# Embedding LayerNorm of a two-layer block: statistics of a token tile in one VectorE pass, tile 0 scaled on ScalarE, one low part on GpSimd

## The reference, cut

```python
def layernorm(x, g, b):
    mu = jnp.mean(xf, axis=-1, keepdims=True)
    var = jnp.mean(jnp.square(xf - mu), axis=-1, keepdims=True)
    y = (xf - mu) * lax.rsqrt(var + LN_EPS) * g + b
...
def hybrid_layer(x, ...):
    proj = x @ w_in
    ...
    return layernorm(DEEPNORM_ALPHA * x + out, ln_g, ln_b)

def first_block(x, ...):
    h = layernorm(x, emb_ln_g, emb_ln_b)
    for l in range(DEPTH):
        h = hybrid_layer(h, ...)
    return h
...
```

## Time and profile before

| | |
|---|---|
| time, median of 3 runs | 2583.37 us (2583.27 to 2583.72) |
| the profiled execution | 2582.42 us |
| its span, first to last instruction | 2580.6 us |
| TensorE busy | 2559.9 us (99%) |
| VectorE busy | 1781.2 us (69%) |
| ScalarE busy | 1360.2 us (53%) |
| GpSimd busy | 16.7 us (1%) |
| DMA queue, share of 16 engines | 52.1% |
| granted TensorE clock, mean | 1.00 |

### The profile page before, as it was taken

The page is one execution under the profiler, slowest core; times in us unless marked ns, Lnnn a source line. Parts: engine busy times, 40 slices in busy tenths (PEclk is TensorE's granted clock), DMA queues, the critical chain, the costliest instruction groups (busy, mean ns, idle before and its releaser), DMA issues.

```text
span 2580.6 us, 39874 instructions
## 1 busy us (share of the span) xinstructions
PE 2559.9 (99%) x14224; PEld 2213.4 (86%) x14224; DVE 1781.2 (69%) x2712; ACT 1360.2 (53%) x2112; POOL 16.7 (1%) x20
## 2 busy tenths in 40 slices
PE   7999999999999999999999999999999999999999
PEld 6888888888888888888888887888888888888888
DVE  8787658777658766556666765678767665666655
ACT  5665565565566444444444554775544444444444
POOL 2000000000000000000000000000000000000000
PEclk9999999999999999999999999999999999999999
DMA  7554455454554555555554564444555545555454
GB/s 296 185 190 177 181 211 228 153 189 177 183 208 163 195 195 178 181 201 191 193 191 164 183 212 163 147 148 170 185 192 186 195 168 189 211 183 193 174 183 164
DMA packets 75435, 482.41 MB, mean 187 GB/s; under 512 B 8384, under 2 KB 10816, under 8 KB 30784
## 3 DMA queue, kind: packets, MB, share of 16 engines
q1 hardware_dynamic: 75328, 481.00, 52.1%
HBM read 477.82 MB, written 2.10 MB: 186 GB/s over the span
## 4 chain that ended last, share of the span: by engine, by line
PE 83%; DVE 1%; ACT 1%; issue 0%; ACTq 0%; DVEq 0%
PE acc L808 45%; PE acc L809 23%; PE acc L814 3%; PE acc L816 3%; PE acc L815 3%; PE score L808 1%; PE score L1080 1%; PE score L809 1%; PE head_ps L1103 0%; DVE low L1527 0%; PE turn_ps L1089 0%; PE head_ps L1104 0%; PE sums L1023 0%; ACT high L1159 0%; ACT L1438 0%
## 5 line engine op out<-in xcount | busy, mean ns | idle before, releaser
L808 PE MATMUL acc<-xs,high 128*128 128x512 f32 x4000 | 1400.6, 396 | 2.5 <-DVE xs L2011 2.3
L1527 DVE TENSOR_TENSOR low<-raw,high 128x1024 fp32r<-128x1024 f32 (+2 forms) x976 | 1079.8, 1124 | 453.4 <-ACT high L1159 429.7
L1159 ACT ACTIVATE high<-raw 128x1024 fp32r<-128x1024 f32 (+2 forms) x976 | 945.2, 976 | 506.3 <-PE acc L809 375.7
L809 PE MATMUL acc<-xs,low 128*128 128x256 f32 x4000 | 1111.2, 278 | 0.0
L808 PEld LDWEIGHTS acc<-xs,high 128*128 128x128 f32 x4000 | 750.3, 188 | 178.2 <-DVE xs L2011 3.2
L809 PEld LDWEIGHTS acc<-xs,low 128*128 128x128 f32 x4000 | 751.7, 188 | 0.6
L808 PE MATMUL acc<-hidden,high 128*128 128x512 f32 x1408 | 490.8, 395 | 0.1
L1198 ACT ACTIVATE lowsum<-acc 128x256 f32<-128x256 f32 x348 | 133.5, 384 | 520.7 <-PE acc L809 520.0
L809 PE MATMUL acc<-hidden,low 128*128 128x256 f32 x1408 | 391.2, 278 | 0.0
L808 PEld LDWEIGHTS acc<-hidden,high 128*128 128x128 f32 x1408 | 264.1, 188 | 62.7 <-DVE low L1527 0.4
L809 PEld LDWEIGHTS acc<-hidden,low 128*128 128x128 f32 x1408 | 264.6, 188 | 0.0
(11 more groups left out here) (374 smaller groups left out, 2017.9 us busy)
## 6 DMA issues: line engine op xcount, KB each, us to landing
raw<-w_up_dram SPq DMA_DIRECT2D x176, 1024.0 KB, 4.8
raw<-w_down_dram SPq DMA_DIRECT2D x128, 704.0 KB, 4.0
raw<-w_in_dram SPq DMA_DIRECT2D x78, 1024.0 KB, 4.8
raw<-w_out_dram SPq DMA_DIRECT2D x32, 1024.0 KB, 4.8
raw<-w_heads_dram SPq DMA_DIRECT2D x24, 1024.0 KB, 4.8
raw<-w_mixout_dram SPq DMA_DIRECT2D x16, 1024.0 KB, 4.8
raw<-w_mem_dram SPq DMA_DIRECT2D x8, 1024.0 KB, 4.8
raw<-w_nat_dram SPq DMA_DIRECT2D x8, 1024.0 KB, 4.8
```

The costliest lines, as they stand in the source:

```text
L808: eng.matmul(bank_, hi, moving, start=start, stop=False)
L809: return eng.matmul(bank_[:, S:2 * S], lo, moving[:, 0:S], start=False, stop=stop)
L1159: eng.activation(high[:, s % SPLIT, to:to + n * P], raw[:, s % RAW, at_:at_ + n * P], ACT.Copy).then_inc((highs_a, highs_b)[piece], 1)
L1527: eng.tensor_tensor(low[:, s % SPLIT, w], raw[:, s % RAW, at_:at_ + n * P], high[:, s % SPLIT, w].bitcast(F32), ALU.subtract).then_inc((lo ...
```

## The change

**Statistics.** VectorE makes mean and variance of a token tile with four `bn_stats` over 512 features each and one `bn_aggr` (`row_moments`); sums, squares and shift are gone from it and from ScalarE. This is done for tile 0 first, up to reciprocal and bias, then for tile 1.

**Scaling.** All four chunks of tile 0 are scaled on ScalarE (`scaled`) while VectorE works on tile 1. Of tile 1, chunks 0 and 1 (`FIRST_ON_DVE`) are scaled on VectorE, the second of them after the affines of bank 1, and chunks 2 and 3 on ScalarE. TensorE transposes the halves of chunks 0 and 1 that belong to tile 0 as soon as they and `par` are there, and the halves of tile 1 after them (`turn_tile`, `turn_first`).

**One low part on GpSimd.** The first piece of slab 1's low part (`low[:, 1, 0:1024]`) is made by GpSimd as its first work, after both first high pieces. It is counted in a semaphore of its own, `emb_low`, for which TensorE waits ahead of the second product (`b` = 0, slab 1). `lows_a` isn't raised for it: the first low piece of slab 2 waits for `emb_low` and raises `lows_a` by 2.

```diff
-ACC_AT = {"emb": 0, "memory": 4, "ln0": 12, "ln1": 30, "memory_heads": 48}
+ACC_AT = {"memory": 0, "ln0": 8, "ln1": 26, "memory_heads": 44}
+FIRST_ON_DVE = 2
...
@@ -890,8 +894,12 @@
                                 eng.wait_ge((lows_a, lows_b)[b // 8], s + n + 1)
                         elif n == 0:
                             wait_split(eng, split_norm(r.name), b)
-                            if b % 8 == 0:
+                            if b % 8 == 0 and (r.name, b) == ("in_a0", 0):
+                                eng.wait_ge(lows_a, 1)
+                            elif b % 8 == 0:
                                 eng.wait_ge((lows_a, lows_b)[b // 8], s + 2)
+                        elif (r.name, b) == ("in_a0", 0):
+                            eng.wait_ge(emb_low, 1)
                         last = product(banks[n], high[:, (s + n) % SPLIT, at_], low[:, (s + n) % SPLIT, at_],
                                        in_mix(r)[:, b, :], b == 0, b == KT - 1)
                         if n:
@@ -1120,11 +1128,11 @@
             def turn_chunk(name, c):
 
                 n = LAYER_NORMS.index(name)
-                if name == "emb" and c == 0:
-                    eng.wait_ge(par_in, 16)
-                eng.wait_ge(z_done, 5 * n + c + TB)
+                if name == "emb":
+                    return turn_first(c)
+                eng.wait_ge(z_done, FIRST_ON_DVE + 5 * (n - 1) + c + TB)
                 if c:
-                    eng.wait_ge(z_second, 3 * n + c)
+                    eng.wait_ge(z_second, 4 - FIRST_ON_DVE + 3 * (n - 1) + c)
                 for j in (2 * c, 2 * c + 1):
                     if j >= 4:
 
@@ -1136,8 +1144,34 @@
                                                  z[:, b, kt * P:(kt + 1) * P], ident)
                     last.then_inc(turned_x, 1)
...
+            def turn_tile(c, b):
+
+                for j in (2 * c, 2 * c + 1):
+                    for m in range(2):
+                        kt = 2 * j + m
+                        last = eng.transpose(turn_banks[j % 4][:, m * S + b * P:m * S + (b + 1) * P],
+                                             z[:, b, kt * P:(kt + 1) * P], ident)
+                    if b:
+                        last.then_inc(turned_x, 1)
+
+            def turn_first(c):
+
+                if c >= 2:
+                    eng.wait_ge(split_l, split_count("emb", 4 * (c - 2) + 3))
+                    eng.wait_ge(emb_first, c + 1)
+                    turn_tile(c, 0)
+                if c < FIRST_ON_DVE:
+                    eng.wait_ge(z_done, c + 1)
+                else:
+                    eng.wait_ge(z_second, c + 1 - FIRST_ON_DVE)
+                turn_tile(c, 1)
+
             def between(name):
                 if name == "in_a0":
+                    eng.wait_ge(par_in, 16)
+                    for c in range(2):
+                        eng.wait_ge(emb_first, c + 1)
+                        turn_tile(c, 0)
                     turn_chunk("emb", 0)
                     turn_chunk("emb", 1)
@@ -1264,18 +1298,22 @@
                     eng.wait_ge(unit_there, 1)
                 eng.activation(dummy[:, :], unit[:, :], ACT.Sqrt)
                 if name == "emb":
-                    whole_squares()
+                    eng.wait_ge(emb_var, 1)
+                    eng.activation(ln_root[:, 0:1], ln_var[:, 0:1], ACT.Sqrt).then_inc(emb_root, 1)
+                    eng.wait_ge(emb_scaled, 1)
+                    for c in range(4):
+                        scaled(0, name, c).then_inc(emb_first, 1)
+                    eng.wait_ge(variance, N_OF[name] + 1)
+                    eng.activation(ln_root[:, 1:2], ln_var[:, 1:2], ACT.Sqrt).then_inc(root, 1)
+                    split_high(0, r, 0, None)
+                    split_high(0, r, 1, None)
+                    eng.wait_ge(par_in, 16)
...
...
+            def scaled(b, name, c):
+                w = slice(512 * c, 512 * (c + 1))
+                return eng.activation(z[:, b, w], token_major(name)[:, b, w], ACT.Identity, bias=ln_bias[:, b:b + 1],
+                                      scale=ln_inv[:, b:b + 1])
+
             def second_scaled(name, c):
                 eng.wait_ge(ln_scaled, LAYER_NORMS.index(name) + 1)
-                w = slice(512 * c, 512 * (c + 1))
-                eng.activation(z[:, 1, w], token_major(name)[:, 1, w], ACT.Identity, bias=ln_bias[:, 1:2], scale=ln_inv[:, 1:2])\
-                    .then_inc(z_second, 1)
-
-            def whole_squares():
-                for n in range(2 * TB):
-                    b, w = n // 2, slice(n % 2 * D // 2, (n % 2 + 1) * D // 2)
-                    eng.wait_ge(x_in[n], 16)
-                    eng.wait_ge(x_first, b + 1)
-                    eng.activation(z[:, b, w], x_tok[:, b, w], ACT.Square, bias=ln_shift[:, b:b + 1],
-                                   accum_out=ln_sums[:, 8 + n:9 + n]).then_inc(accumulated, 1)
+                scaled(1, name, c).then_inc(z_second, 1)
@@ -1493,6 +1526,9 @@
                 steps_done += 1
                 eng.wait_ge(pool_order, steps_done)
 
+            eng.wait_ge(highs_a, 2)
+            eng.tensor_tensor(low[:, 1, 0:8 * P], raw[:, 1, 0:8 * P], high[:, 1, 0:8 * P].bitcast(F32),
+                              ALU.subtract).then_inc(emb_low, 1)
...
                 eng.wait_ge((highs_a, highs_b)[piece], val(s + 1, 4, i))
+                both = (s, piece) == (2, 0)
+                if both:
+                    eng.wait_ge(emb_low, 1)
                 eng.tensor_tensor(low[:, s % SPLIT, w], raw[:, s % RAW, at_:at_ + n * P], high[:, s % SPLIT, w].bitcast(F32),
-                                  ALU.subtract).then_inc((lows_a, lows_b)[piece], 1)
+                                  ALU.subtract).then_inc((lows_a, lows_b)[piece], 2 if both else 1)
...
                 c = N_OF[name]
                 if name == "emb":
-                    whole_sums()
-                    eng.tensor_reduce(ln_total[:, 0:TB], ln_sums[:, 0:8].rearrange("p (n c) -> p n c", c=4), AX.X,
-                                      ALU.add).then_inc(x_sums, 1)
-                    eng.wait_ge(x_sums, 1)
-                    eng.tensor_scalar(ln_offset, ln_total[:, 0:TB], -1.0 / D, None, ALU.mult)
-                    step_(eng.scalar_tensor_tensor(out=ln_mean, in0=ln_total[:, 0:TB], scalar=1.0 / D, in1=ln_shift,
-                                                   op0=ALU.mult, op1=ALU.add))
-                    step_(eng.tensor_tensor(ln_square, ln_mean, ln_mean, ALU.mult))
-                    eng.wait_ge(accumulated, accumulations(name, 2 * TB))
-                    step_(eng.tensor_reduce(ln_total[:, TB:2 * TB], ln_sums[:, 8:12].rearrange("p (n c) -> p n c", c=2), AX.X,
-                                            ALU.add))
-                    step_(eng.tensor_scalar(ln_var, ln_total[:, TB:2 * TB], 1.0 / D, LN_EPS, ALU.mult, ALU.add))
-                    eng.tensor_tensor(ln_var, ln_var, ln_square, ALU.subtract).then_inc(variance, 1)
-                    eng.wait_ge(root, c + 1)
-                    step_(eng.reciprocal(ln_inv, ln_root))
-                    eng.tensor_tensor(ln_bias, ln_offset, ln_inv, ALU.mult).then_inc(ln_scaled, 1)
+                    for b in range(TB):
+                        row_moments(b)
+                        one = slice(b, b + 1)
+                        eng.tensor_scalar(ln_var[:, one], emb_stat[:, b, 1:2], LN_EPS, None, ALU.add)\
+                            .then_inc((emb_var, variance)[b], 1)
+                        step_(eng.tensor_scalar(ln_offset[:, one], emb_stat[:, b, 0:1], -1.0, None, ALU.mult))
+                        eng.wait_ge((emb_root, root)[b], 1)
+                        step_(eng.reciprocal(ln_inv[:, one], ln_root[:, one]))
+                        eng.tensor_tensor(ln_bias[:, one], ln_offset[:, one], ln_inv[:, one], ALU.mult)\
+                            .then_inc((emb_scaled, ln_scaled)[b], 1)
                     return
@@ -1967,22 +2000,17 @@
             def z_chunk(name, c):
 
                 w = slice(512 * c, 512 * (c + 1))
-                for b in range(1 if c else TB):
+                for b in [1] if name == "emb" else range(1 if c else TB):
                     eng.tensor_scalar(z[:, b, w], token_major(name)[:, b, w], ln_offset[:, b:b + 1], ln_inv[:, b:b + 1],
                                       ALU.add, ALU.mult).then_inc(z_done, 1)
 
-            def whole_sums():
-                for n in range(4 * TB):
-                    b, c = n // 4, n % 4
+            def row_moments(b):
+                for c in range(4):
                     if c % 2 == 0:
-                        eng.wait_ge(x_in[n // 2], 16)
-                    ins = eng.tensor_reduce(ln_sums[:, n:n + 1], x_tok[:, b, 512 * c:512 * (c + 1)], AX.X, ALU.add)
-                    if c == 0:
-                        step_(ins)
-                        eng.tensor_scalar(ln_shift[:, b:b + 1], ln_sums[:, n:n + 1], -1.0 / 512, None, ALU.mult)\
-                            .then_inc(x_first, 1)
```

(11 more changed lines are left out.)

16 lines of the change are left out of this document (7 added, 9 removed).

## The result

The changed kernel takes **2593.46 us** in the median of its runs (2589.99 to 2608.87, and one launch of 13.8 ms, which is an outlier and not counted below), the kernel before 2583.37 beside it. The ratio is 1.0041, 95% interval 1.0027 to 1.0056: slower by 10 us (0.4%), where 2581.9 was forecast and 2580.9 to 2584.0 was the range. The profiled execution of after took 2590.99, its span is 2589.2.

The account below looks back on a forecast made before the run. TensorE was taken as the bound, busy 2559.9 of 2580.6 us, with gains only from its early stops; -1.5 for `b` = 8 and 0 elsewhere took the median from 2583.37 to 2581.9, range 2580.9 to 2584.0.

Parts of the forecast that it names:

- Sum. -1.5 for `b` = 8, 0 for `rows`, 0 for the rest: Whole kernel: the terms added up, taking the profiled execution from 2582.42 to 2580.9 and the median to 2581.9 us.
- `b` = 8: TensorE's product after its last early stop: to start at 26.1 instead of 27.60, 1.5 us earlier.
- `rows`: Load queued behind slab 5: issued at 31.4, landing at 44.5, VectorE waiting 4.1 us, 0.6 slack before TensorE's tile 5.
- the zero for the rest: Everything besides the start and the `rows` load: claimed to change the time by 0.
- My rivals: Four other outcomes: late `rows` 0.16, slow GpSimd part 0.12 or 0.02 with a load, slow first products 0.08, slow BN_STATS 0.03.
- rival 3: TensorE slow at its first products, eight pairs taking twice 2.9 us, 0.9 of it hidden: 2583.9; chance 0.08.
- Statistics: VectorE's embedding norm: each BN_STATS 0.69 us, and the root moving from 12.1 to 11.4.
- ScalarE: Second high part held by its DMA until 13.1, ending at 14.2 as before; affines start at 14.1, not 14.95.
- First product: TensorE's first product at 16.9 instead of 18.09, with 0.2 added for contention with GpSimd.
- GpSimd's part: Low part of slab 1 from 14.3, bounds 2.9 to 5.1 us, taken as 3.3; second product waits 0.3.
- Rival 4: BN_STATS no gain at 1.38 us each, first product near 21.5: 2586.7; chance 0.03.

Follow-up runs that it names:

- experiment 5: Four kernels that shift where tiles lie in memory, compared with the kernel before: ratios 1.0084, 1.0002, 1.0008 and 1.0044.
- tiles_unused: The kernel before with the two small tiles (224 bytes) allocated between `ln_stat` and `dummy` and never used: 2602.67 us, ratio 1.0084.
- after_again: The changed kernel, unaltered, run again beside the kernel before: 2606.91 us, ratio 1.0063.

## Why the prediction was wrong, point by point

**The step that failed** is "Sum. -1.5 for `b` = 8, 0 for `rows`, 0 for the rest", and in it the zero for the rest. I had gone through instructions, waits and queues, and passed over two lines of the change, the allocations of `emb_parts` and `emb_stat` (the excerpt of the diff ahead of the prediction doesn't have them; they are the two lines shown under experiment 5). They have no instruction and no wait, but they displace `par` and every tile behind `ln_stat` by 224 bytes. So it isn't true that the change touches only the first 30 us. `tiles_unused` shows these lines alone to be worth +19 in the median of its four launches (ratio 1.0084). In its profile only the first feed-forward layer is slow, and from the scalings to the first gain behind the layer it takes 653.0 us, 11.5 more than the 641.5 of before. The forecast also took the rate of the products as a constant, and the trace of before holds both rates. The groups of its stretch 1422 to 1560, against its 394 and 277 ns above:

```profile
L808 PE MATMUL acc<-hidden,high 128*128 128x512 f32 x313 | 111.0, 399 | 0.1
L809 PE MATMUL acc<-hidden,low 128*128 128x256 f32 x313 | 87.9, 281 | 0.0
```

My rivals all asked which wait ends later, and TensorE that is busy longer was among them only as rival 3, at the start.

**Statistics.** Right: 0.63 each (0.69 taken), aggregate 0.26, and the second root at 11.10 (11.4).

**ScalarE.** Wrong by 0.9, in the kernel's favour: the second `high` part was to be held by its DMA until 13.1. The two ran back to back, 11.20 to 13.19. `raw` of slab 1 landed at 11.70, where I had it at 13.04 from the 9.5 to landing. That landing belonged to one execution: over the 20 profiles it lies between 11.70 and 13.09, and the profile that I read has one of the two latest.

**First product.** 16.82 against 16.9, but by two errors that cancel, so the hit is luck. ScalarE was earlier, and VectorE's second `z` chunk, 0.54 alone, took 1.60 beside GpSimd's low part. I had put 0.2 for that contention; it cost 1.1.

**GpSimd's part.** 2.44 long (3.3 taken, 2.9 to 5.1 as bounds), from 13.28 to 15.7. The quarter-width row times four was too long even at its lower end. The Trainium skill, GPSIMD Engine Reference, § 3.1, has 4497 ns for twice the width; half of that, an estimate from the page, is 2.25, and the trace agrees within 0.2 us. The 6 us that the Trainium skill, GPSIMD Engine Reference, § 2.1, adds to a first call do not show in the trace, 2.44 being this engine's first tensor_tensor. Nobody waited for the part itself. Rival 4 has a small slip in its sum: a first product at 21.5 is 4.6 behind 16.9 and gives 2586.5, not 2586.7. With BN_STATS at 0.63 the rival did not arise.

**`b` = 8.** 25.05 against 26.1: -2.55 and not -1.5. But more than half of the 2.55 is luck of the loads. Where the first piece of slab 1 landed by 12.3, `b` = 8 lies at 26.6 to 26.9 in the six profiles with the old start, and at 25.05 to 26.2 in the five with the new one, 1.2 less in the mean. Over all profiles of either start it is 26.87 in seven and 25.96 in eight, 0.9 less. So the forecast of -1.5 was somewhat too good, where this one profile makes it look too cautious. There was one more loss, which rival 3 named: the first products still came 0.64 apart (17.61, 18.25) and not 0.35, under a granted clock of 1.00, the level of 2.4 GHz, and the eight ahead of the transposes took 3.8, not 2.9. TensorE no longer stops on the way to `b` = 8, so these 0.9 are in the 25.05 and not hidden, as I had said they would be.

**`rows`.** Issued at 30.57, VectorE waits 4.91 (4.1 said), and TensorE stops 0.39 ahead of 47.87 where 0.6 of slack was left by the sum. The place was right and the size off by 1.0, about as much as TensorE came earlier to it. `after_again`, the same kernel, has no such stop. At 60 us it is 2.6 ahead of before.

**Sum of these.** -2.6 at 60 us (start, loads and draws together), -3.2 at 775, +11.7 in the feed-forward layer gives +8.5 at 1428.

## What to carry to other kernels

When a bound engine gets slower without a wait and without a drop of its clock, compare how many of its instructions fit in equal stretches of both kernels before looking for something late; and give every launch's time, since a median over a mixture of 2582, 2595 and 2608 hides it. A new tile ahead of others is part of a change: put it behind the last one, so that every other tile stays where it was, before the rest is judged (here 256 bytes of padding did no harm either). And a landing time read from one profile is a draw too: take it from several. A gain of some us at the start of a kernel is worth measuring only when such a draw of 12 us is held still.
